# Inner levels of a delta-rule scan made half as wide, and the order of work changed in two mixer stages of a 16-stage fp32 kernel

## The reference, cut to what matters

```
z = gelu(h @ w_in + b_in); u, v = split(z)        # 2048 wide each
v = layer_norm(v) * v_gain
s = einsum('gij,bcjgd->bcigd', masked w_s, v) + b_s   # 8 groups of 256 columns, blocks of 128 tokens
out = (u * s) @ w_out
```

```
S_t = S_{t-1} diag(w_t) + (S_{t-1} a_t) b_t^T + v_t k_t^T ;  y_t = S_t r_t
out = (norm(y) * lnx + bonus) * g @ w_out
```

## Time and profile before

| | |
|---|---|
| time, median of 3 runs | 2408.85 us (2408.38 to 2411.97) |
| profiled execution, own time | 2401.35 us |
| its span | 2399.5 us |
| mean granted clock of PE | 0.983 |
| stage 1, from the first step of "in" to that of "out" | about 207 to 313 us of the span |
| stage 5, from the first product of "k" to the next stage | about 776 to 1046 us of the span |

### The profile page before, as it was taken

How to read it: one execution, slowest core, us unless ns; L and a number is a source line. 1 busy time by engine, 2 the same in 40 slices (tenths; PEclk the granted TensorE clock), 3 DMA queues, 4 the chain that set the end, 5 groups by cost and what they waited for, 6 DMA issues and landing times.

```text
span 2399.5 us, 32778 instructions
## 1 busy us (share of the span) xinstructions
PE 2278.4 (95%) x12883; PEld 1840.0 (77%) x12883; DVE 1493.5 (62%) x2069; ACT 1158.4 (48%) x1672; POOL 175.0 (7%) x288
## 2 busy tenths in 40 slices
PE   8999999999998988889999999998999999969998
PEld 6888778887887557768887888866888788748886
DVE  5656657647665867576557656655655765647655
ACT  5445545446544453244455445444445544545444
POOL 1001000001000010410011000001000000041001
PEclk9999999999999999989999999999999999989999
DMA  7556636554646420056555655513555555506552
GB/s 243 191 182 216 216 122 220 180 192 156 213 165 213 156 99 4 21 179 193 177 200 167 192 185 197 178 36 116 188 184 193 176 186 185 194 10 205 177 184 105
DMA packets 289751, 395.68 MB, mean 165 GB/s; under 512 B 11672, under 2 KB 193248, under 8 KB 289600
## 3 DMA queue, kind: packets, MB, share of 16 engines
q1 hardware_dynamic: 284800, 377.33, 47.4%
q0 software_dynamic: 4656, 16.20, 2.0%
q10 hardware_dynamic: 144, 0.07, 0.0%
HBM read 392.50 MB, written 1.05 MB: 164 GB/s over the span
## 4 chain that ended last, share of the span: by engine, by line
PE 75%; DVE 6%; ACT 4%; issue 2%; POOL 1%; DMA 0%; DVEq 0%; POOLq 0%; ACTq 0%; SPq 0%
PE bank L490 22%; PE bank L492 22%; PE bank L491 22%; PE bank L516 1%; PE bank L1320 1%; ACT wh L605 1%; PE bank L504 1%; ACT JUNK L612 1%; DVE wl L789 1%; DVE TMP L827 1%; DVE qPS L1677 0%; DVE H L847 0%; PE bank L1322 0%; PE bank L1347 0%; PE bank L1334 0%
## 5 line engine op out<-in xcount | busy, mean ns | idle before, releaser
L789 DVE TENSOR_TENSOR wl<-raw,wh 128x1024 fp32r<-128x1024 f32 x708 | 859.4, 1224 | 592.0 <-ACT wh L605 591.1
L605 ACT ACTIVATE wh<-raw 128x1024 fp32r<-128x1024 f32 x708 | 743.9, 1058 | 671.3 <-PE bank L492 641.7
L490 PE MATMUL bank<-wh,XH 128*128 128x512 f32 x2000 | 802.6, 401 | 26.8 <-DVE XL L806 6.1
L491 PE MATMUL bank<-wl,XH 128*128 128x512 f32 x2000 | 784.5, 392 | 0.0
L492 PE MATMUL bank<-wh,XL 128*128 128x512 f32 x2000 | 784.3, 392 | 0.0
L490 PEld LDWEIGHTS bank<-wh,XH 128*128 128x128 f32 x2000 | 379.1, 190 | 116.2 <-issue 20.5
L492 PEld LDWEIGHTS bank<-wh,XL 128*128 128x128 f32 x2000 | 378.6, 189 | 82.2
L491 PEld LDWEIGHTS bank<-wl,XH 128*128 128x128 f32 x2000 | 379.7, 190 | 74.4 <-issue 0.5
L490 PE MATMUL bank<-wh,AH 128*128 128x512 f32 x704 | 276.0, 392 | 0.0
L492 PE MATMUL bank<-wh,AL 128*128 128x512 f32 x704 | 274.1, 389 | 0.0
L491 PE MATMUL bank<-wl,AH 128*128 128x512 f32 x704 | 274.1, 389 | 0.0
(11 more groups left out here) (317 smaller groups left out, 1771.0 us busy)
## 6 DMA issues: line engine op xcount, KB each, us to landing
raw<-in_ffn_w_dram SPq DMA_DIRECT2D x184, 512.0 KB, 4.6
raw<-in_ffn_wi_dram SPq DMA_DIRECT2D x176, 512.0 KB, 4.6
raw<-in_ffn_w_dram SPq DMA_DIRECT2D x40, 1024.0 KB, 4.9
raw<-in_ffn_wo_dram SPq DMA_DIRECT2D x40, 1024.0 KB, 4.9
raw<-in_a_wqkv_dram SPq DMA_DIRECT2D x18, 1024.0 KB, 4.8
raw<-in_a_w_in_dram SPq DMA_DIRECT2D x16, 1024.0 KB, 5.7
raw<-in_b_w_in_dram SPq DMA_DIRECT2D x12, 1024.0 KB, 4.9
bc<-in_norm_g_dram POOLq DMA_DIRECT2D x16, 512.0 KB, 5.4
```

What stands on the lines that cost most here:

```text
L490: pe.e.matmul(o, a, h, start=(k == 0), stop=False)
L491: pe.e.matmul(o, a, l, start=False, stop=False)
L605: act.e.activation(self.wh[j % N_W][:, 0:p.size], self.raw[p.chunk % N_RAW][:, p.at:p.at + p.size], ACT.Copy).then_inc(*self.rounded.up(j))
L789: dve.e.tensor_tensor(self.wl[j % N_W][:, 0:p.size], self.raw[p.chunk % N_RAW][:, p.at:p.at + p.size], self.wh[j % N_W][:, 0:p.size].bitca ...
```

## The change

Three places change; the arithmetic of the reference stays.

1. Stage 1: the mix of group c and the transposes of y are put between the steps of blocks 5, 6 and 7 (mix c ahead of the 2nd step of block 5 + c, transposes 2c and 2c + 1 ahead of its 10th and 11th), mix 3 ahead of step 127, and the last two transposes ahead of steps 9 and 10 of "out". The mix uses banks 6 and 7 and no longer counts in `n_pairs`. On DVE the product with u of group c stands ahead of the leave at the first part of block 5 + c, the leave of y ahead of that of its third part.
2. Stage 5, input: ACT rounds parts 5 and 6 of "k" after the first `act_normed`; DVE leaves parts 3 and 4 inside `dve_out`, after t = 0, and parts 5 and 6 singly between the mixtures of t = 1; PE transposes t = 1 at steps 2 and 4 instead of 6 and 7.
3. Stage 5, scan: `dve_keys_rated` of t = 1 moves from part 7 to part 5 of "v"; the leave of part 5 of "out" comes after the first "tt", that of part 6 after "fin" of (1, 0); both "tt" of t = 0 stand first; the levels work on the 32 columns that a level can change instead of 64, with one predicated copy for each x instead of one for both.

```diff
-            self.round(act, p.j + N_W)
+            if tail < 2 or not self.before_rwkv(n):
+                self.round(act, p.j + N_W)
...
+            if t == 0 and self.before_rwkv(n):
+                for p in layer.parts[first:first + 2]:
+                    self.leave(dve, p.j + N_W)
...
+            for c in range(3):
+                if step == 16 * (5 + c) + 2:
+                    self.pe_gmlp_mix(pe, c)
+                if step in (16 * (5 + c) + 10, 16 * (5 + c) + 11):
+                    self.pe_gmlp_turn(pe, 2 * c + step % 16 - 10)
+            if step == 16 * 7 + 15:
+                self.pe_gmlp_mix(pe, 3)
+
+        def beside_out(step):
+            if step in (9, 10):
+                self.pe_gmlp_turn(pe, step - 3)
...
+    def pe_gmlp_mix(self, pe, g2):
+
+        self.place["pair", ("mix", g2)] = 3
+        for t in range(T):
+            bank = self.take_bank(pe, 6 + t, (self.made, "y", g2, t))
+            pe.wait_ge(self.made, "ws")
+            pe.wait_ge(self.made, "v", g2 // 2, t)
...
+            if i >= 20 and i % 4 == 2:
+                self.act_gmlp_turned(act, i // 4 - 5)
...
+            if i >= 20 and i % 4 == 0:
+                self.dve_gmlp_gated(dve, i // 4 - 5)
+            if i >= 20 and i % 4 == 2:
+                self.dve_gmlp_turned(dve, i // 4 - 5)
...
     def pe_beside_k(self, pe, step):
-        if step in (6, 7):
-            self.pe_turn_h(pe, 1, step - 6)
+        if step in (2, 4):
+            self.pe_turn_h(pe, 1, step // 2 - 1)
...
         self.act_normed(act, 0)
+        for j in range(5, 7):
+            self.round(act, self.layers[n, "k"].parts[j].j)
...
-        for j in range(3, 5):
-            self.leave(dve, first + j)
-        for q in range(2):
-            self.dve_turned_h(dve, n, 1, q)
-            self.dve_mix(dve, 1, 1, q)
-        for q in range(2):
-            self.dve_mix_low(dve, 1, 1, q)
-        for j in range(5, 7):
-            self.leave(dve, first + j)
+        self.dve_turned_h(dve, n, 1, 0)
+        self.dve_mix(dve, 1, 1, 0)
+        self.dve_turned_h(dve, n, 1, 1)
+        self.leave(dve, first + 5)
+        self.dve_mix_low(dve, 1, 1, 0)
+        self.dve_mix(dve, 1, 1, 1)
+        self.leave(dve, first + 6)
+        self.dve_mix_low(dve, 1, 1, 1)
...
-                self.leave(dve, p.j + N_W)
+                if name != "v" or i < 6:
+                    self.leave(dve, p.j + N_W)
...
-        if i == 7:
+        if i == 5:
             self.dve_keys_rated(dve, 1)
...
+        steps += [("tt", 0, 0), ("tt", 0, 1)]
         for o in range(2):
-            steps += [("tt", 0, o), ("gram", 0, o), ("krv", 0, o)]
+            steps += [("gram", 0, o), ("krv", 0, o)]
...
-                m = pe.e.matmul(banks[e][self.HALF[x], r * HD:(r + 1) * HD], L[h, r, x, :], Y[h, r, x, :], start=True,
-                                stop=True)
+                m = pe.e.matmul(banks[e][self.HALF[x], r * 32:(r + 1) * 32].rearrange("p (g b) -> p g b", b=2 ** lv),
+                                L[h, r, x, :], self.scan_right(Y[h, r, x, :], lv), start=True, stop=True)
...
-        act.wait_ge(self.left, self.layers[n, "out"].parts[6].j)
...
+                act.wait_ge(self.left, self.layers[n, "out"].parts[5].j)
                 self.act_scan_halves(act, "krv", "rh", *a)
...
+                if (t, o) == (0, 0):
+                    self.leave(dve, self.layers[n, "out"].parts[5].j)
+            elif kind == "fin":
+                if tuple(a) == (1, 0):
+                    self.leave(dve, self.layers[n, "out"].parts[6].j)
...
+                b = 2 ** lv
+                mask = self.scan_right(self.rMK[:, 4 + lv, :].bitcast(mybir.dt.uint16), lv)
+                for x in range(2):
+                    m = dve.e.copy_predicated(
+                        self.sY[o][:, :, x, :].rearrange("p r (g i b) -> p r g i b", i=2, b=b)[:, :, :, 1, :],
+                        mask.unsqueeze(1).broadcast_to([P, 4, 32 // b, b]),
+                        self.scan_banks("y", t, o, lv)[:, x * 512:x * 512 + 128].rearrange("p (r g b) -> p r g b", r=4, b=b))
+                m.then_inc(*self.made.up("y", t, o, lv))
...
+    def scan_right(self, x, lv):
+
+        return x.rearrange("p (g i b) -> p g i b", i=2, b=2 ** lv)[:, :, 1, :]
```

## The result

The changed kernel takes 2393.97 us (median of 4 executions, 2388.43 to 2396.55), the kernel before beside it 2408.61 us (median of 4, 2408.36 to 2411.97). The ratio is 0.9927, with a 95% interval from 0.9909 to 0.9945: 0.7% faster. The medians differ by 14.6 us; the ratio alone would make it -17.6 us, its interval -21.9 to -13.2. The forecast was 2394.3, faster.

What follows compares the result with a forecast made beforehand. PE was taken as the bound, busy 2278.4 of 2399.5 us, so only its idle or slow time or its work could be saved. Terms of +3.0, -6.1, -8.5, -3.7 and +0.8 gave -14.5: 2394.3 us, range 2385.5 to 2403.

Steps and rivals of the forecast that it cites:

- The sum: All five terms together: 3.0 - 6.1 - 8.5 - 3.7 + 0.8 = -14.5 us, from 2408.85 to 2394.3.
- Stage 1: Moved mixes and transposes: PE waits for v, then about 5.2 us for y; +3 us, bounds +1.5 and +4.5.
- slow restart: PE runs slowly after a hole of about 4 us or more, priced at another 1.5 us.
- Input: Stage 5 input: "k" starts 0.8 earlier, step 11's 3.9 us hole and 1.5 behind it go; -6.1 us.
- Scan start: Stage 5, transposes to first level: shorter DVE queue before the copy of the keys; -8.5 us, bounds -6 and -9.5.
- the bank's wait: At the scan, the second transposes wait for ACT's copy out of their pair of banks, a loss of 1.5 us.
- Rival (c): Part of the scan or input gain is given back, 5 to 8 us less, 2400 to 2402; chance 0.16.
- Levels: Scan levels on 32 columns: DVE's copies shorten, PE's pace stays with the weight loads; -3.7 us, bounds -1 and -10.
- Part 6's leave: After the levels, a 1.22 us leave before "seen" of (2) in DVE's chain; +0.8 us, bounds 0 and 1.3.

Runs made afterwards that it cites:

- e1: Only the stage 1 part (mixes and transposes beside the first layer), laid on the kernel before: 2410.29 us, ratio 1.0001.
- e11: e7 with the scan's first steps in the order of the kernel before, leaves and rated keys as in e7: 2399.03 us, ratio 0.9945 against the kernel before.
- the whole again: The whole changed kernel measured once more, beside the others on one chip: 2397.16 us, ratio 0.9944 against the kernel before.
- e3: Only the scan's start, with part 6's leave moved and mixes still counted in the bank rotation, laid on the kernel before: 2399.97 us, ratio 0.9948.
- e5: The whole change without the stage 1 part: 2392.44 us, ratio 0.9927 against the kernel before.
- e7: The whole change with the bank-pair rotation advanced by one and part 6's leave behind the last "seen": 2390.25 us, ratio 0.9909 against the kernel before.
- e8: e7 with stage 1's mixes and transposes placed anew, some steps between a mix and the transposes ahead: 2389.15 us, ratio 0.9913 against the kernel before.
- e9: e7 without the stage 1 part: 2393.03 us, ratio 0.9920 against the kernel before.
- e10: The whole change with the copy to sW as wide as before, 256 columns a half: one execution, 2399.13 us.

## Why the prediction was right, term by term

- **The sum.** -14.5 forecast; the medians differ by 14.6 and 14.3, and the ratios give -17.6 and -13.5. From the profiles, with T, L and F of the pair before and changed, K and S as differences of means: +0.6 - 0.8 - 5.0 - 6.9 - 3.3 + 2.7 = -12.7, inside the second interval and half a microsecond outside the first. Stage 1 came 2.4 below its term, the others together 4.2 short of theirs. These errors offset each other in part, and single executions scatter by some 15 us, so it is luck that the forecast lies 0.3 us from the median. The signs of all five terms are right, and that is not luck: each has its mechanism in the traces. In the one pair of traces 274.3 - 261.7 = 12.6 is won between the start of "k" and the second tail of stage 5; that the spans differ by 7.0 only is mostly R, 4.7 longer though the change doesn't touch it.
- **Stage 1, +3: mechanism right, size too large.** Both stalls and their releasers came as described, and the turns in "out" cost 26.1 - 24.9 = 1.2, predicted 1.3. But the holes are 6.5 us, not 8.2: the slow passes behind the first lie ahead of the second and shorten it (in e1, e11 and the whole again, where they last longer, the second is 2.3 to 2.4). The step that failed is the addition of 1.5 for a slow restart to a base of 313.06 taken from one execution, whose stage 1 has no time at the lower clock: S is 131.9 there. It is 133.3 to 135.1 in four of the other five kernels with the old stage 1, which have such time at its end; the mean of the six is 133.7, against 134.3 of the six with the placing of the change. The slow restart comes in all six new ones, but in four of the six old ones too. So it is +0.6 instead of +3, under its lower bound of 1.5; each mean has a standard error of about 0.5, and e1's ratio cannot tell it from nothing.
- **Input, -6.1: right, -5.9.** In the pair of traces K is 5.1 shorter (112.1 to 107.0), and "k" starts 13.1 instead of 13.9 after the tail on DVE at 763.44, -0.8: -5.9. The mean of K over ten kernels with the new order is 109.3, over four with the old one 114.3, or 113.0 without e1, whose K of 118.2 has a granted clock of 0.90 against 0.94 to 0.96. With the hole for `b_g2` taken out the means are 105.9 and 111.1. The prediction had PE driving everything from step 11 to the end of "v"; that hole is in between. It swallowed nothing, because SP's issue moved with the rest: 68 us behind the start of "k" instead of 73.
- **Scan start, -8.5: -6.9, mechanism right.** The first gram came at +5.2 (predicted 5.1) and krv at +9.65 (9.4); then the second gram took 2.87 us for 62 passes, 1.93 to 1.97 at the higher clock, and its krv came at +15.9 instead of +14.0. The sum had the bank's wait, and left out the low clock in the second gram. In e3, e5, e7, e8 and e9, with the other rotation, a wait of 0.50 stands in place of the 1.41, the low clock doesn't come, and T is 13.8: the wait costs 3.1 with what comes behind it. Rival (c) came in this form, with a wait for the bank and a slow stretch behind it, but smaller than its 5 to 8. Why the clock falls there in each trace with that wait is not shown.
- **Levels, -3.7: -3.3.** t = 0 gives 0.9, t = 1 2.4. PE kept its pace: 222 against 224 ns. The prediction argued this from the weight loads, which stay at 134 ns; no run changes the loads, so that they set the pace is not shown. The Trainium skill, TensorEngine Tiling (Array Packing), section Performance Considerations, says that a free size under about 60 takes as long as 60. The trace agrees at 32 against 64 columns.
- **Part 6's leave, +0.8: +2.4 to +2.7, outside its bounds.** F is 12.4 to 12.8 in five kernels with the leave in this place (13.5 in e10), and 9.9 to 10.6 in the eight others. The step that failed is the price of 1.22 us from the group's mean: beside POOL the leave takes 2.29, and only its first half microsecond lies under PE's last pass for "seen". The Trainium skill, SBUF — State Buffer, section on its two separate sides, says that a VectorE operation with two operands in SBUF and a GpSimd one that reads SBUF exclude each other on a shared pair of ports. The trace fits this, with 2.29 beside POOL and 1.23 in e7 after POOL had ended; POOL's L2706, which starts beside the leave, takes 2.13, and 1.27 in e7 without it. No run isolates the ports.

The best versions are e7 and e8, at 0.991; between them and e9 the measurement cannot choose.

## What to carry to other kernels

Price a hole by what stands in front of it in the queue of the engine that ends it: at the scan 7.8 of 10 us were two leaves and some products ahead of one copy, and the order on PE was worth 2.3. When work is moved beside other work, follow its banks as well as its data: the mixes that were placed right behind transposes in the same two banks cost 11 us. Look at the whole way between two places before saying that a shift arrives: a load of 32 rows, issued late, held PE for 2.3 to 4.5 us in all kernels here, and the change leaves it in. And before a term is taken from one trace, look at how much an untouched stretch of the same length moves from one execution to the next.

## What was not expected of the hardware

The same holes leave PE slow in one execution and not in another. Behind a hole of 2.46 us at 575.05 the kernel before went on at 0.39 us a pass; behind one of 2.17 us at 575.39 the changed kernel had passes of 0.63 until 579.3; between two instructions of DVE that stand at 572.6 and 580.7 in before it lost 1.4 us more. The granted clock of the whole span moved between 0.976 and 0.984 over the profiled executions, and the untouched R by 7.4 us. What decides it is open.

The load of `b_g2` let PE go on 6.0 to 8.3 us after its issue, with the same issue code in all fourteen traces and nothing else for PE to do. In the ten kernels with the new order K goes with that wait: 107.0 to 108.3 where it is 2.3 to 2.7 us, 110.6 to 111.9 where it is 4.3 to 4.5. What makes it longer in some executions is open too.
